# Order of the front of a hybrid S5, Hyena and FFN block: the filter's taps before the squares, and the last four adaLN blocks between the first steps of the k-outer input projection

## The reference

```python
silu_c, silu_cc = jax.nn.silu(c), jax.nn.silu(c_ctx)[None]
# adaLN: one vector each for x and ctx, 6 parts of 2048
mod_x = silu_c @ w_ada + b_ada
mod_c = silu_cc @ w_ada + b_ada
h_c = rms_norm(ctx, norm_mix) * (1 + cscale_mix) + cshift_mix
u_c = h_c @ w_in[:, :S5_WIDTH]
h_x = rms_norm(x, norm_mix) * (1 + scale_mix) + shift_mix
p_x = h_x @ w_in          # [S5 input | Hyena v, x0, x1 | two gates]

def hyena_filters(n, lp):  # two sine layers, a linear one, a decaying window
    h = sin(f1_freq * (feats @ f1_w + f1_b))
    h = sin(f2_freq * (h @ f2_w + f2_b))
    h = (h @ f3_w).reshape(n, 2, HY_WIDTH)
    return h * exp(-t * abs(hy_decay))
# then: S5 scans seeded by the context, Hyena long convolution with the filter's
# spectrum, gated merge, output projection, SwiGLU FFN, final RMSNorm
```

## Time and profile before

| | us |
|---|---|
| median of 3 runs (lowest, highest) | 2972.01 (2969.21, 2976.94) |
| profiled execution: its own time | 2966.34 |
| its span | 2964.5 |
| PE busy / DVE / ACT / POOL in the span | 2894.2 / 1501.6 / 834.8 / 191.7 |
| PE busy in the first 64 us | 38.2 |
| PE waits for adaLN loads, in total | 15.6 |
| PE waits for squares / for the first load | 4.5 / 3.9 |
| PE waits for a weight split, at 121.6 and at 238.1 | 3.5 and 3.5 |

### The profile page before, as it was taken

The page is one execution under the profiler, slowest core; times in us unless marked ns, Lnnn a source line. Parts: engine busy times, 40 slices in busy tenths (PEclk is TensorE's granted clock), DMA queues, the critical chain, the costliest instruction groups (busy, mean ns, idle before and its releaser), DMA issues.

```text
span 2964.5 us, 33640 instructions
## 1 busy us (share of the span) xinstructions
PE 2894.2 (98%) x14204; PEld 2380.2 (80%) x14204; DVE 1501.6 (51%) x2044; ACT 834.8 (28%) x1220; POOL 191.7 (6%) x337
## 2 busy tenths in 40 slices
PE   6999999999999999999999999999999999999997
PEld 2587888888888888787878888888888888888886
DVE  5645665985553777877765423222232223323245
ACT  4331433224442522221232222222222222222221
POOL 0000000001233001111000000000000000000000
PEclk9999999999999999999999999999999999999998
DMA  9644232334446438876536523333333333332333
GB/s 408 275 112 103 98 101 98 121 124 130 131 143 195 172 128 275 297 286 239 185 113 203 167 87 98 103 97 100 88 103 100 93 100 88 104 100 93 95 93 110
DMA packets 122744, 426.54 MB, mean 144 GB/s; under 512 B 15985, under 2 KB 16241, under 8 KB 119266
## 3 DMA queue, kind: packets, MB, share of 16 engines
q1 hardware_dynamic: 84082, 300.87, 31.6%
q0 software_dynamic: 32752, 111.99, 11.5%
q10 hardware_dynamic: 5760, 11.54, 1.0%
HBM read 396.12 MB, written 28.18 MB: 143 GB/s over the span
## 4 chain that ended last, share of the span: by engine, by line
PE 90%; DMA 5%; DVE 3%; ACT 1%; issue 1%; SPq 0%; ACTq 0%; DVEq 0%
PE ps L1784 26%; PE ps L1786 26%; PE ps L1785 26%; DMA ada_mix<-in_w_ac 2%; PE ps L1754 2%; DMA hw_raw<-in_w_in 1%; PE ps L1865 1%; PE ps L1828 1%; PE ps L1801 1%; DMA hw_raw<-in_w_glu 1%; PE ps L1755 1%; PE ps L1692 1%; PE ps L1671 1%; DMA hw_raw<-in_w_out 1%; PE ps L1802 1%
## 5 line engine op out<-in xcount | busy, mean ns | idle before, releaser
L964 DVE TENSOR_TENSOR hw_lo<-hw_raw,hw_hi 128x1024 fp32r<-128x1024 f32 (+2 forms) x512 | 583.6, 1141 | 1251.8 <-ACT hw_hi L577 1250.0
L577 ACT ACTIVATE hw_hi<-hw_raw 128x1024 fp32r<-128x1024 f32 (+2 forms) x512 | 507.9, 993 | 1557.1 <-DMA hw_raw<-in_w_fi 576.6
L1784 PE MATMUL ps<-h_hi,hw_hi 128*128 128x512 f32 x2272 | 889.4, 391 | 0.0
L1786 PE MATMUL ps<-h_hi,hw_lo 128*128 128x512 f32 x2272 | 884.7, 389 | 0.0
L1785 PE MATMUL ps<-h_lo,hw_hi 128*128 128x512 f32 x2272 | 883.9, 389 | 0.0
L1786 PEld LDWEIGHTS ps<-h_hi,hw_lo 128*128 128x128 f32 x2272 | 426.4, 188 | 89.5
L1785 PEld LDWEIGHTS ps<-h_lo,hw_hi 128*128 128x128 f32 x2272 | 426.8, 188 | 87.3
L1784 PEld LDWEIGHTS ps<-h_hi,hw_hi 128*128 128x128 f32 x2272 | 426.8, 188 | 87.2 <-issue 0.4
L1784 PE MATMUL ps<-act_hi,hw_hi 128*128 128x512 f32 x704 | 274.0, 389 | 0.0
L1786 PE MATMUL ps<-act_hi,hw_lo 128*128 128x512 f32 x704 | 273.9, 389 | 0.0
L1785 PE MATMUL ps<-act_lo,hw_hi 128*128 128x512 f32 x704 | 273.9, 389 | 0.0
(11 more groups left out here) (313 smaller groups left out, 2881.2 us busy)
## 6 DMA issues: line engine op xcount, KB each, us to landing
hw_raw<-in_w_fi SPq DMA_DIRECT2D x176, 512.0 KB, 3.5
hw_raw<-in_w_in SPq DMA_DIRECT2D x128, 512.0 KB, 3.7
ada1m<-in_w_ar POOLq DMA_DIRECT2D x128, 512.0 KB, 5.1
ada_mix<-in_w_ac SPq DMA_DIRECT2D x16, 2048.0 KB, 13.1
hw_raw<-in_w_fo SPq DMA_DIRECT2D x64, 384.0 KB, 3.1
hw_raw<-in_w_fo SPq DMA_DIRECT2D x64, 320.0 KB, 2.9
hw_raw<-in_w_glu SPq DMA_DIRECT2D x32, 512.0 KB, 4.7
hw_raw<-in_w_out SPq DMA_DIRECT2D x32, 512.0 KB, 4.5
```

Source lines behind the costliest of these rows:

```text
L577: act.activation(hw_hi[slot(n)][:, 0:width(n)], hw_raw[slot(n)][:, 0:width(n)], ACT.Copy).then_inc(w_hi, 1)
L964: tt(hw_lo[s][:, 0:w], hw_raw[s][:, 0:w], hw_hi[s][:, 0:w].bitcast(F32), SUB).then_inc(w_lo, 1)
L1784: mm(out, wh(k), xh[:, k0 + k, :], start=first and k == 0, stop=False)
L1786: ins = mm(out, wl(k), xh[:, k0 + k, :], start=False, stop=last and k == nk - 1)
```

## The change

Six pieces, all of them order; no operation is added or taken away.

1. SP issues decay, its row and the filter's third weights before adaLN block 0; ctx is issued by SP behind block 4 instead of by POOL at the start, and x behind it.
2. On PE the front has the taps groups first: adaLN blocks 0 to 4 and the four taps groups, then all squares of ctx, then the spectrum steps. On DVE and ACT the same order.
3. The spectrum steps take adaLN blocks 5 to 11 along, from step 1 on, and the squares of x in steps 1 to 4.
4. The k-outer steps 0 to 3 take blocks 12 to 15, one behind each.
5. h is prepared one tile ahead of PE (k + 1) instead of two (k + 2), and only tile 0 before the loop.
6. ACT splits weight piece 10 between the second and the third unit store instead of behind the fourth; the first sine comes before decay's absolute value.

The diff, cut to its core:

```diff
@@ -364,25 +364,26 @@
...
             sp.dma_start(vecs[:, :], vecs_d).then_inc(s_vec, 16)
-            ada_mix(0)
             sp.dma_start(hyb[:, :], hyb_d).then_inc(s_dec, 16)
...
             sp.dma_start(f3w[:, :], f3w_d).then_inc(s_f3w, 16)
-            ada_mix(1)
-            x_in(0)
-            x_in(1)
-            ada_mix(2)
-            x_in(2)
-            x_in(3)
+            for c in range(3):
+                ada_mix(c)
             tab_in(1)
...
             ada_mix(3)
+            ada_mix(4)
+            sp.dma_start(c_raw[:, :, :], ctx_d).then_inc(s_ctx, 16)
+            for g in range(4):
+                x_in(g)
             tab_in(0)
-            for c in range(4, 13):
+            for c in range(5, 11):
                 ada_mix(c)
             sp.wait_ge(s_squ, 2 * KT)
-            for c in range(13, 16):
-                weights(c - 13)
+            for c in range(11, 14):
+                weights(c - 11)
+                ada_mix(c)
+            for c in range(14, KT):
                 ada_mix(c)
@@ -437,7 +438,6 @@
...
             pool.dma_start(postab[:, :, :], postab_d).then_inc(s_pos, 16)
-            pool.dma_start(c_raw[:, :, :], ctx_d).then_inc(s_ctx, 16)
 
@@ -623,55 +623,51 @@
...
 
+            filter_sin(0)
             act.wait_ge(s_dec, 32)
             act.activation(decay[:, :], decay[:, :], ACT.Abs).then_inc(s_absd, 1)
-            filter_sin(0)
             act.wait_ge(s_absd, 1)
...
             windows(1)
-            for k in range(4):
-                square(k)
             ada_rows(1)
-            for k in range(4, 8):
-                square(k)
             windows(2)
-            for k in range(8, KT):
-                square(k)
             ada_rows(2)
...
             windows(3)
-            for c in range(4, 7):
-                ada_rows(c)
+            ada_rows(4)
+            for k in range(KT):
+                square(k)
             for st in range(8):
-                if st < 4:
-                    for k in range(KT + 4 * st, KT + 4 * st + 4):
+                if 1 <= st < 5:
+                    for k in range(KT + 4 * st - 4, KT + 4 * st):
                         square(k)
-                if st == 3:
+                if st == 4:
                     act.wait_ge(s_squ, 2 * KT)
...
                     act.activation(ssr[:, SEQ:SEQ + CTX], ps[5][:, 0:CTX], ACT.Copy).then_inc(s_row, 1)
-                ada_rows(7 + st)
-                if st == 4:
+                if st:
+                    ada_rows(4 + st)
+                if st == 5:
                     act.wait_ge(s_var, 1)
                     act.activation(rt6[:, 2, :], rt6[:, 1, :], ACT.Sqrt).then_inc(s_sqrt, 1)
-                if st == 5:
+                if st == 6:
                     act.wait_ge(s_rsp, 1)
...
                     act.activation(rs_c[:, :], ps[4][:, 0:CTX], ACT.Copy).then_inc(s_rs, 1)
-                if st >= 6:
-                    h_hi_tile(st - 6)
-                    hc_hi_tile(st - 6)
+                if st == 7:
+                    h_hi_tile(0)
+                    hc_hi_tile(0)
             act.wait_ge(kf_free, 8)
...
             for k in range(KT):
-                if k < KT - 2:
-                    h_hi_tile(k + 2)
-                    hc_hi_tile(k + 2)
-                if k == 0:
-                    ada_rows(15)
+                if k < KT - 1:
+                    h_hi_tile(k + 1)
+                    hc_hi_tile(k + 1)
+                if k < 4:
+                    ada_rows(12 + k)
                 if k >= 2 and k % 2 == 0:
@@ -699,8 +695,11 @@
...
                 for e in range(U_K if u == U_K else 1):
+                    if e == 2:
+                        split_hi(2 * u + 2)
                     store_u(e if u == U_K else u - 1)
-                split_hi(2 * u + 2)
+                if u > U_K:
+                    split_hi(2 * u + 2)
                 if u == U_K:
@@ -1072,25 +1071,22 @@
...
             mix_coefficients(1)
-            taps(1)
-            mix_coefficients(2)
-            mix_coefficients(3)
-            taps(2)
-            mix_coefficients(4)
-            taps(3)
-            mix_coefficients(5)
+            for t in range(1, 4):
+                taps(t)
+                mix_coefficients(t + 1)
             a, b, c, e, r = (rt6[:, j, :] for j in range(5))
             for st in range(8):
-                if st < 4:
-                    for k in range(4 * st, 4 * st + 4):
+                if 1 <= st < 5:
+                    for k in range(4 * st - 4, 4 * st):
                         position(k)
-                if st == 4:
+                if st == 5:
                     dve.wait_ge(s_ss, 1)
...
                 filter_fold(st)
-                mix_coefficients(6 + st)
-                if st == 4:
+                if st >= 2:
+                    mix_coefficients(3 + st)
+                if st == 5:
                     dve.wait_ge(s_sqrt, 1)
@@ -1099,17 +1095,16 @@
...
                         ts(dg[:, j, :], ident[:, :], rt6[:, 4, j:j + 1], None, MUL).then_inc(s_dg, 1)
-                if st == 6:
+                if st == 7:
                     dve.wait_ge(s_rs, 2)
-                if st >= 6:
-                    block(st - 6)
+                    block(0)
             for n in range(3):
...
             for k in range(KT):
-                if k < 2:
-                    mix_coefficients(14 + k)
-                if k < KT - 2:
-                    block(k + 2)
+                if k < 5:
+                    mix_coefficients(11 + k)
+                if k < KT - 1:
+                    block(k + 1)
                 if k >= 2 and k % 2 == 0:
@@ -1702,38 +1697,32 @@
...
             taps(0)
-            for k in range(8):
+            mix_columns(0)
+            ada_mix(2)
+            mix_columns(1)
+            for t in range(1, 4):
+                taps(t)
+                if t < 3:
+                    ada_mix(t + 2)
+                mix_columns(t + 1)
+            for k in range(KT):
                 sums(k)
-            mix_columns(0)
-            mix_columns(1)
-            taps(1)
-            for k in range(8, KT):
-                sums(k)
-            ada_mix(2)
-            ada_mix(3)
-            taps(2)
-            mix_columns(2)
-            mix_columns(3)
-            ada_mix(4)
-            taps(3)
-            mix_columns(4)
-            ada_mix(5)
-            mix_columns(5)
-            ada_mix(6)
             pe.wait_ge(s_tap, 4)
             for st in range(8):
-                if st == 4:
+                if st == 5:
                     pe.wait_ge(s_row, 1)
...
                 spectrum_of_filter(st)
-                mix_columns(6 + st)
-                if st < 4:
-                    for k in range(KT + 4 * st, KT + 4 * st + 4):
+                if st >= 2:
+                    mix_columns(3 + st)
+                if 1 <= st < 5:
+                    for k in range(KT + 4 * st - 4, KT + 4 * st):
                         sums(k)
-                ada_mix(7 + st)
-                if st == 5:
+                if st:
+                    ada_mix(4 + st)
+                if st == 6:
                     for j in range(6):
@@ -1759,11 +1748,11 @@
...
             for k in range(KT):
-                if k < 2:
-                    mix_columns(14 + k)
+                if k < 5:
+                    mix_columns(11 + k)
                 units_by_k(k)
-                if k == 0:
-                    ada_mix(15)
+                if k < 4:
+                    ada_mix(12 + k)
 
```

## The result

| | before | after |
|---|---|---|
| median of the timed runs, us (20 each) | 2970.98 | 2977.75 (2971.88 to 2982.76) |
| ratio after / before, 95% interval | | 1.0021 [1.0014, 1.0029] |
| profiled execution, its own time, us | 2966.34 | 2977.63 |
| span, us | 2964.5 | 2975.8 |

One of the 20 runs before took 3651.94 us, and the ratio leaves it out, as it is taken over fast runs alone. The change costs 0.21%, some 6.2 us: inside the band of "no change" (0.3%), on its slow side, and 3 us above the forecast of 2974.7. As a difference, 2.7 us were forecast. The two traces differ by 11.3 us, more than the medians, since the execution traced of before was 4.6 us faster than its own median and that of after stood at its median. So the traces are used to find places, and the medians to weigh them.

What follows compares the result with a forecast made beforehand. PE, 98% busy, bounds the kernel; only work ahead of the first spectrum step can shrink. Front -7.4, loop +8.6, lookahead +0.8, split +0.7 sum to +2.7 on 2972.0: 2974.7 us, range 2965 to 2982.

Steps and rivals of the forecast that it cites:

- Block 0 at 14.3: Front: adaLN block 0 starts on PE at 14.3 instead of 15.5, ctx's load gone (-4.9), decay and f3w ahead (+3.7).
- Layer to product: Front: from the second filter layer to the taps product takes 7.3 us, so that product starts at 25.2, 2.5 earlier.
- Then a column pair (0.6) and the taps-1 product (2.0): Front: after PE's idle 7 us and block 2 (3.6), these follow, and DVE gets taps 1 at 42.0.
- T0: First spectrum product, end of the front: forecast at 58.0, 6.2 us earlier; bounds 56.3 to 59.5.
- The steps: Eight spectrum steps: 2.7 us less, so 50.0, plus 0.6 for squares of x and 1.2 for low clock.
- The way to k0: Last block to first k-outer product: 4.4 us instead of 4.7, putting that product at 114.2, 7.4 earlier.
- The loop: K-outer loop: three more adaLN blocks at 2.88 us each, uncovered by other work, cost 8.6 us.
- The lookahead: K-outer loop: h prepared for k + 1 instead of k + 2 costs 0.8 us, bounds 0 to 6.
- The rival of 12 us: K-outer loop: PE waits for h at k = 8, 10, 12, 14 and pays low clock; 12 us, 2986; chance 0.10.
- The split: Unit stores: weight 10's split delays the third store and POOL's gather, costing 0.7 us; bounds -0.5 to 1.5.
- The wait near 238 us: PE's second wait for a weight split: stays 3.5 us or more; a later gather comes out there one for one.
- faster: the loads were the bound: Front: better filter-chain overlap brings the first spectrum step at about 47, 11 us more gain, 2964; chance 0.08.

Runs made afterwards that it cites:

- e6: Changed kernel with each loop block's column pair behind the next k's products and its coefficients behind the next h block; 2971.97 us, ratio to before 1.0008.
- second trace: The changed kernel run once more without any edit, for another trace; 2975.07 us, ratio to before 1.0015.
- e4: Kernel before with only adaLN blocks 12 to 15 moved between the first k-outer steps; 2978.00 us, ratio 1.0031.
- e10: e7 with block(0) before fold 7 on DVE and h prepared two tiles ahead again, ACT's order matching; 2965.54 us, ratio to before 0.9984.
- e5: Kernel before with only the split of weight piece 10 moved between the second and third unit store; 2970.61 us, ratio 1.0001.
- e1: Changed kernel with adaLN block 0 loaded ahead of decay and f3w again; 2970.06 us, ratio to before 0.9993.
- e8: e4 with DVE and ACT doing block(0) before fold 6 and block(1) behind the first weight split; 2974.52 us, ratio to before 1.0016.
- e2: Changed kernel with block 0's column pair and coefficients ahead of taps 0 on PE and DVE; 2968.99 us, ratio to before 0.9996.
- e3: Changed kernel with the edits of e1 and e2 together; 2966.59 us, ratio to before 0.9988.
- e7: Changed kernel with the edits of e1, e2 and e6, and the split of piece 10 back behind the stores; 2963.63 us, ratio to before 0.9980.

## Why the prediction was right, and where it was not

The call (no measurable change, 2974.7 in a range of 2965 to 2982) held, with 2977.75. The change itself was priced too low: +2.7 forecast, +6.2 measured by the ratio. Step by step:

- **Block 0 at 14.3.** 14.46, 14.65 and 14.41 in three traces with these loads, and 16.78 in the first trace of the changed kernel. Right, but the load scatters by over 2 us, which the bounds left out.
- **Layer to product, 7.3 us; DVE's taps 0, 7.3 us; the gap of 7 us behind it; taps 1 to 3, 16.0 us.** Measured 7.35, 7.3, 7.41 and 15.85. All right.
- **"Then a column pair (0.6) and the taps-1 product (2.0)": this is the step of the front that failed.** I priced the block behind the gap at the low clock (3.6 us, measured 3.59) and what stood behind it at the full one. They took 1.02 and 3.78 us. With taps 0's own product at 3.44 instead of 2.74, T0 came 3.0 us later than forecast from the clock alone; with block 0 it is 5.3, and 63.27 lies outside the bounds of 56.3 to 59.5. It is no fixed price: in e6, the same front, the pair and the product took what I had priced, and T0 is 59.16, inside the bounds.
- **The steps: 51.8 us forecast, 51.86 measured.** This is luck. I had added 0.6 for the squares of step 1 and 1.2 for a low clock. The clock took nothing (granted 1.00 from 63.27 on), and step 1 took 1.9 us more than its work at the rates of the other steps.
- **The way to k0: 4.4 us forecast, 4.9 measured.** Near in size, but the path was another. I counted from PE's last block; the chain of waits goes over DVE's fold and its store. k0: 120.04 instead of 114.2.
- **The loop: 3 x 2.88 = 8.6 us.** The three steps that gained a block take 7.2 us instead of 4.2: +9.1 in all. The price was right, with 0.2 us more in each of them around the block.
- **The lookahead: 0.8, bounds 0 to 6.** The steps k = 4 to 12 take 1.2 us longer in the changed kernel (up to 4.49 each instead of 4.16), and 1.8 in its second trace, where one takes 5.21. e4, which keeps the lookahead of two, shows 0.8 of such excess as well, so some 0.4 to 1.0 are the lookahead's. e10 takes them away. The rival of 12 us falls.
- **The split: 0.7.** Not borne out: the gather comes 0 to 0.2 us later by it (e5).
- **The wait near 238 us: it did not go**, it is 4.7 us instead of 3.5, and it passes the gather's delay on: gather +10.3, split +11.3. The 1.0 between them is scatter of the load beside the gather; from the gather to PE's product there are 34.1 to 36.3 us in the thirteen traces.
- **The upper end of the sum.** By the bounds of the terms it is not +9 but +10.7 (1.5 for T0, 0.5 for the clock, 5.2 for the lookahead and 0.8 for the split above the forecast of 2.7), so 2982.7, beyond the range given.

From k0 to the gather the changed kernel takes 11.8 us more in one trace and 11.5 in the other, with 10.1 forecast. Ahead of k0 it gains 1.6 and 3.7 us against the trace of before. That trace was an early one: e5, which has the front of before, has k0 at 124.37, 2.8 us later, and against it the gain is 4.3 and 6.5. The medians point there too: 6.2 us of loss with some 11.6 paid behind k0 leave 5.4 gained in front (an estimate from these numbers), where 7.4 were forecast. So of the 3.5 us by which the forecast of the difference was low, some 2 are the front and 1.5 the loop. The range held because that is small against its width of 17 us.

What I had not seen at all is what decides k0. I wrote that "the steps are PE's sum of work" and that "the loads don't bind". In the steps PE waits for no load, that much is true. But in the kernel before, DVE's folds, held by stores that crawl beside the loads, already end later than PE's work: PE is done at 118.06 and waits 3.55 us. e4 shows what follows: 7 us of PE's work leave, and k0 gains 1. The store stands in the chain ahead of k0 in seven of the thirteen traces (before, after, e1, e4, e5, e6 and e8). In the second trace of the changed kernel and in e2, e3 and e7 PE's last spectrum products decide. That is why moving blocks from the steps to the loop can't pay in the old front, and pays in the changed one only as far as T0, and with it the folds, come earlier. The Trainium skill, DMA: Bandwidth & Descriptors, section Queues, rings and completion order, says that a DMA engine takes turns between its queues packet by packet; the traces agree in so far as a store of 512 KB from POOL's queue took 11.0 to 12.3 us where it decided k0 beside SP's loads (7.3 in e8), and 3.2 us where few loads ran.

The rival "faster: the loads were the bound" (T0 at 47) describes what e3 and e7 come near to, with T0 at 50.4, and not what the change does: it needed the gap gone.

## What to carry to other kernels

Before moving work off the bottleneck engine ahead of a join, follow back every arm of the join and see which one decides. Here it was not PE's work but DVE's folds and the stores that free their buffers, so taking work off PE gained nothing by itself, while the price at the new place was paid in full. When a reordering opens a gap of several microseconds on TensorE, price a case in which not only the instruction behind it runs at the low clock but those after it as well (8.2 us of work in one trace, the first 3.4 us alone in another with the same order), and look whether a few small instructions that the gap waits for can go first (e2: 6 us for one step moved). The median minus the gather's time in one trace lies between 2760 and 2768 us in all thirteen rows of the table while the gather moves by 15 us; the median minus the traced span lies between -4.9 and +6.5. So a mark ahead of a long steady stretch weighs an edit somewhat better than the span of a single trace. It doesn't weigh one of a few us: e1's gather is 6.3 us behind that of before, and its ratio is 0.9993.

## What the runs showed of the hardware

- After a gap of 7.41 us TensorE was granted 0.50 (1.2 GHz) for the next 8.2 us, in which it was idle for 0.04. A pair took 1.02 instead of 0.61 us and the taps product 3.78 instead of 1.99. In e6, after a gap of 6.98 us at the same place, the first 3.4 us of work were slow, and the same pair and product took 0.61 and 1.99.
- A store of 512 KB took 3.16 us while the DMA engines moved 166 GB/s and 11.03 us while they moved 423 (changed kernel, at 69.41 and 102.34).
- From 4 to 8 us the DMA engines moved 346 to 414 GB/s where decay and f3w were ahead of block 0, and 335 to 452 where block 0 was ahead, against 424 in the steps. So the slow start isn't tied to what stands first, and its cause is open.
- One k of the loop takes 4.16 us in some traces and 4.24 in others, flat through the loop (e8 4.16, e4 4.24), though the work is the same: over 12 such steps 1 us that no edit made.
